# First tiles and first weight slices prepared one stage ahead in a three-layer transformer kernel on one core

## The reference

```
for l in range(2):                                   # first block
    mod = silu(c) @ w_ada[l] + b_ada[l]              # shift, scale, gate
    h = layer_norm(x) * (1 + scale) + shift
    u, v, z_a, q, k, val, z_b, q_idx, k_idx, w_idx = split(h @ w_in[l])
    y_a = silu(z_a) * spatial_gating_unit(u, v, ...)
    # q, k, q_idx, k_idx get a rotary embedding
    y_b = silu(z_b) * sparse_attention(q, k, val, q_idx, k_idx, w_idx)   # top 256 keys by index score
    x = layer_norm(ALPHA * x + gate * (concat(y_a, y_b) @ w_out[l]), ln_g, ln_b)
h = rms_norm(x, norm_pre)                            # second block
aq, ak, av, az, dq, dk, dv, db, da, dz, ga, gn = split(h @ w_in_2)
# dense attention on rms-normed, rotated aq, ak; a bidirectional gated delta rule on dq, dk, dv;
# both gated, summed, multiplied by w_out_2, normalised and added to x; a gated side input p is added last
```

## Time and profile before

| | |
|---|---|
| median of three runs | 3689.68 us |
| the profiled execution | 3680.2 us |
| its span (first to last instruction) | 3678.2 us |
| TensorE matmul busy | 3138.2 us, 85% |
| VectorE busy | 2146.1 us, 58% |
| ScalarE busy | 1372.8 us, 37% |
| GpSimd busy | 1140.9 us, 31% |
| bytes moved by DMA | 306.24 MB, 83 GB/s over the span |

### The profile page before, as it was taken

How to read it: one execution, slowest core, us unless ns; L and a number is a source line. 1 busy time by engine, 2 the same in 40 slices (tenths; PEclk the granted TensorE clock), 3 DMA queues, 4 the chain that set the end, 5 groups by cost and what they waited for, 6 DMA issues and landing times. The chain is left out here.

```text
span 3678.2 us, 43621 instructions
## 1 busy us (share of the span) xinstructions
PE 3138.2 (85%) x15729; PEld 2536.9 (69%) x15729; DVE 2146.1 (58%) x4123; ACT 1372.8 (37%) x2729; POOL 1140.9 (31%) x1248
## 2 busy tenths in 40 slices
PE   4899878868998788598998998968878688899788
PEld 3578645645776456487887886768867688688567
DVE  5699787556996876576772005457755577101223
ACT  1366345213763551235662212444323443121221
POOL 1236311221462113422004242225422344423310
PEclk9999999989998999799999999989989799899899
DMA  5322411531223125410002113123231331412511
GB/s 199 123 78 92 131 44 55 172 127 52 78 90 128 44 63 175 150 41 6 1 1 95 49 63 117 31 56 89 48 109 29 73 80 46 158 49 103 174 66 46
DMA packets 233337, 306.24 MB, mean 83 GB/s; under 512 B 40959, under 2 KB 149247, under 8 KB 230945
## 3 DMA queue, kind: packets, MB, share of 16 engines
q1 hardware_dynamic: 221602, 282.47, 24.8%
q10 hardware_dynamic: 11520, 20.98, 1.6%
HBM read 243.48 MB, written 59.90 MB: 82 GB/s over the span
## 5 line engine op out<-in xcount | busy, mean ns | idle before, releaser
L669 PE MATMUL psum<-qs,hT 128*128 128x512 f32 x1344 | 308.7, 391 | 9.5 <-POOL qs L756 9.3
L2342 PE MATMUL psum<-hTs,cws 128*128 128x512 f32 x1152 | 284.3, 408 | 33.2 <-POOL hTs L2589 29.5
L669 PEld LDWEIGHTS psum<-qs,hT 128*128 128x128 f32 x1344 | 252.5, 189 | 65.6 <-POOL qs L756 7.6
L2342 PEld LDWEIGHTS psum<-hTs,cws 128*128 128x128 f32 x1152 | 226.3, 198 | 82.8 <-POOL hTs L2589 30.3
L2093 PE MATMUL psum<-bhsn,bringn 128*128 128x512 f32 x1152 | 264.8, 392 | 14.1 <-POOL bringn L2138 13.3
L2093 PE MATMUL psum<-bhsa,bringa 128*128 128x512 f32 x1152 | 264.1, 392 | 9.4 <-POOL bringa L2138 9.4
L2093 PEld LDWEIGHTS psum<-bhsn,bringn 128*128 128x128 f32 x1152 | 217.7, 189 | 61.1 <-issue 13.6
L2093 PEld LDWEIGHTS psum<-bhsa,bringa 128*128 128x128 f32 x1152 | 218.1, 189 | 55.4 <-issue 9.8
L1403 PE MATMUL psum<-w_out,oys 128*128 128x512 f32 x768 | 180.0, 396 | 27.2 <-DVE w_out L1462 25.6
L1403 PEld LDWEIGHTS psum<-w_out,oys 128*128 128x128 f32 x768 | 146.6, 192 | 61.3 <-DVE w_out L1462 27.2
L836 DVE TENSOR_SCALAR_CACHE_REDUCE junk<-score,cand 128x384 uint8<-128x384 f32 x248 | 186.8, 810 | 2.2
(11 more groups left out here) (449 smaller groups left out, 6998.0 us busy)
## 6 DMA issues: line engine op xcount, KB each, us to landing
stg<-in_w_in SPq DMA_DIRECT2D x96, 256.0 KB, 2.7
wa<-in_w_ada SPq DMA_DIRECT2D x32, 512.0 KB, 3.5
pj<-ptmp ACTq DMA_DIRECT2D x64, 256.0 KB, 2.2
dlb<-blocks SPq DMA_DIRECT2D x32, 512.0 KB
dlb<-in_w_in SPq DMA_DIRECT2D x24, 512.0 KB, 3.9
wa<-in_w_ada SPq DMA_DIRECT2D x8, 1024.0 KB, 8.5
oyf<-yTd SPq DMA_DIRECT2D x16, 512.0 KB, 4.7
ostg<-in_w_out SPq DMA_DIRECT2D x16, 512.0 KB, 6.0
```

What stands on the lines that cost most here:

```text
L669: mm = pe.matmul(bank(m), lhs, rhs, start=(kc == 0 and x == 0), stop=(kc == KC - 1 and x == 2))
L2342: mm = pe.matmul(ps[:, u % 4, :], ws[c % 2][:, a, kc, :], hs[:, b, kc, half * HALF:(half + 1) * HALF], start=(kc == 0 and x == 0), stop=(k ...
```

## The change

The first tile of an index-inputs stage and that stage's weights are now fetched, normalised, turned and modulated in the stage ahead of it. For layer 0 that is the conditioning stage, for layer 1 the first-output stage of layer 0. A new class `FirstTile` holds the buffers and the steps. The first two tiles of the attention inputs and the 8 slices of their first weight chunk are prepared in the first-output stage of layer 1, by a new class `InputsAhead`; there, tile 0 is fully split and its turned form stored, and tile 1 is only normalised. Names are kept alive across the stages by an `ExitStack` called `early`, on the other side of the memory.

With it go: in the first-output stage of layer 1 the buffers `yf` and `ys` are three in place of four; the attention inputs have four staging buffers in place of three; the two `wa` buffers of the index inputs lie in `h.score`; and `recycle_semaphores` runs ahead of each first-output stage and once more after the second, three times in place of two.

```diff
+class FirstTile:
+    def load_w(self, sp):
+        w = self.k.t["w_in"][self.l].rearrange("(k p) n -> p k n", p=P)
+        sp.dma_start(self.w_qi[:, :, :], w[:, :, QI0:KI0]).then_inc(self.s_w, 16)
+        sp.dma_start(self.w_sm[:, :, 0:2 * HD], w[:, :, K0:ZB0]).then_inc(self.s_w, 16)
+        sp.dma_start(self.w_sm[:, :, 2 * HD:], w[:, :, KI0:D_IN]).then_inc(self.s_w, 16)
...
+class InputsAhead:
+    def load_w(self, sp, v):
+        if v >= 4:
+            sp.wait_ge(self.s_wlo, v - 3)
+        sp.dma_start(self.raw[v % 4], self.k.t["w_in_2"][0, v * P:(v + 1) * P, AK0:AK0 + HALF]).then_inc(self.s_w[v % 4], 16)
...
 stage_conditioning
             for kc in range(2, KC):
                 cd.load(sp, kc)
+            first.load_x(sp, k.t["x"][0])
+            first.load_w(sp)
...
             cd.sum_columns(pe, 0, ps[:, 5, 0:2 * KC])
+            first.turn(pe)
...
+            act.wait_ge(cd.s_kept, 1)
+            first.modulate(act)
...
             for kc in range(2, KC):
                 cd.accumulate(dve, kc)
+            first.stats(dve)
+            first.normalise(dve)
...
 stage_first_output
+        YF = YS = 3 if ahead else 4
...
+                if first and n == 3:
+                    sp.wait_ge(s_st[0], 16)
+                    first.load_x(sp, x_out)
+                    first.load_w(sp)
+                if ahead and n == 3:
+                    sp.wait_ge(s_st[0], 16)
+                    sp.wait_ge(s_wlo, KC)
+                    ahead.load_x(sp, 0)
+                    ahead.load_npre(sp)
+                    for v in range(4):
+                        ahead.load_w(sp, v)
+                if ahead and n == 4:
+                    sp.wait_ge(s_st[1], 16)
+                    ahead.load_x(sp, 1)
+                if ahead and n in (5, 6):
+                    ahead.load_w(sp, 2 * n - 6)
+                    ahead.load_w(sp, 2 * n - 5)
...
             def y_hi(n):
                 act.wait_ge(s_yl[n % YF], 16 * (n // YF + 1))
-                if n >= SLOTS:
-                    act.wait_ge(s_mm, n - SLOTS + 1)
+                if n >= YS:
+                    act.wait_ge(s_mm, n - YS + 1)
...
+                if ahead and 3 <= n < 7:
+                    ahead.w_lo(pool, 2 * n - 6)
+                    ahead.w_lo(pool, 2 * n - 5)
+                if ahead and 4 <= n < 6:
+                    ahead.rstd(pool, n - 4)
...
 stage_attention_inputs
-    SLICES, STAGING = CH * KC, 3
+    SLICES, STAGING = CH * KC, 4
...
-            turn_x(0)
             turn_x(1)
...
                 for kc in range(KC):
-                    if n == 0:
-                        pe.wait_ge(s_wlo, c * KC + kc + 1)
+                    if n == 0 and c:
+                        pe.wait_ge(s_wlo, (c - 1) * KC + kc + 1)
...
 build
-                stage_first_output(k, l, x_in, t["x1"] if l == 0 else t["x2"])
                 k.recycle_semaphores()
+                if l + 1 < DEPTH:
+                    tile0, inputs = FirstTile(k, early, l + 1), None
+                else:
+                    tile0, inputs = None, InputsAhead(k, early)
+                stage_first_output(k, l, x_in, t["x1"] if l == 0 else t["x2"], tile0, inputs)
+            k.recycle_semaphores()
```

More of the change, by code:

```diff
@@ L225, in stage_conditioning @@
+def stage_conditioning(k, first):
     nc, t, ps = k.nc, k.t, k.ps
@@ L255, in _ @@
             cd.clear(pool)
+            first.rstd(pool)
         @block.tensor
@@ L312, in stage_index_inputs @@
     with ExitStack() as ctx:
-        xb = [h.score[:, i * D:(i + 1) * D] for i in range(XB)]
+        xb = [first.x[:, :], h.score[:, 0:D]]
         xn = xb
-        hf = [h.score[:, (2 + i) * D:(3 + i) * D].rearrange("p (c q) -> p c q", c=KC) for i in range(2)]
-        w_qi = k.sb(ctx, f"w_qi_{l}", [P, KC, HALF])
-        w_sm = k.sb(ctx, f"w_sm_{l}", [P, KC, SMALL])
+        hf = [first.hf[:, :, :], h.score[:, D:2 * D].rearrange("p (c q) -> p c q", c=KC)]
+        wa = [h.score[:, (2 + i) * D:(3 + i) * D] for i in range(2)]
+        w_qi, w_sm = first.w_qi, first.w_sm
         st = k.sb(ctx, f"st_{l}", [P, 2, 2, 6])
@@ L407, in project @@
                 if n == 0:
-                    pe.wait_ge(s_w, 48)
+                    pe.wait_ge(first.s_w, 48)
                 if n >= 2:
@@ L1334, in _, with stage_first_output @@
                 gate(v)
-def stage_first_output(k, l, x_in, x_out):
+def stage_first_output(k, l, x_in, x_out, first, ahead):
     nc, t, ps = k.nc, k.t, k.ps
@@ L1376, in _ @@
                     s_wl[kc % STAGING], 16)
-            for n in range(LEAD, YF):
+            for n in range(LEAD, LEAD + 1):
                 load_y(n)
@@ L1420, in _ @@
                     part(n, kc)
+            if first:
+                pe.wait_ge(s_g, NT - SLOTS + 1)
+                first.turn(pe)
+            if ahead:
+                pe.wait_ge(s_g, NT - SLOTS + 1)
+                ahead.turn(pe)
         @block.scalar
@@ L1436, in _ @@
                 y_hi(n)
+                if ahead and n == NT - 2:
+                    ahead.square(act, 0)
+                    for v in range(4):
+                        ahead.w_hi(act, v)
+            if first:
+                first.modulate(act)
+            if ahead:
+                ahead.square(act, 1)
+                for v in range(4, KC):
+                    ahead.w_hi(act, v)
+                ahead.scale(act)
         @block.gpsimd
@@ L1464, in _ @@
             for n in range(NT + 1):
+                if first and n == 6:
+                    first.stats(dve)
+                if first and n == 7:
+                    first.normalise(dve)
+                if ahead and 6 <= n < NT:
+                    ahead.normalise(dve, n - 6)
                 if n < NT:
@@ L1486, in _, with stage_attention_inputs @@
                                              ALU.add).then_inc(s_o, 1)
-def stage_attention_inputs(k, a):
+            if ahead:
+                ahead.split(dve)
+def stage_attention_inputs(k, a, ahead):
     nc, t, ps = k.nc, k.t, k.ps
```

341 lines of the change are left out of this document (218 added, 123 removed).

## The result

Beside each other on one chip the changed kernel took 3652.38 us (median of 4 runs, 3644.80 to 3660.35) and the kernel before 3691.09 us (4 runs, 3685.44 to 3700.91): a ratio of 0.9893, 95% interval 0.9862 to 0.9923, so 1.1% faster. The forecast was 3652 us, faster. The profiled execution of the changed kernel took 3650.61 us with a span of 3648.7 us, 29.5 us less than the span of before.

What follows compares the result with a forecast made beforehand. TensorE, busy for 85% of the span, was taken as the bound, with gains only where it stands still or runs at half rate. 7.2 + 8.2 + (26.4 - 2 - 1.8) = 38.0 us off 3689.7 gave 3651.7, range 3637 to 3669.

Steps and rivals of the forecast that it cites:

- parts 4 and 5: First output of layer 1, a loss of 2 us; attention inputs up to the last low part, a gain of 26.4 us.
- parts 2 and 3: First output of layer 0 ends 3.5 us later; layer 1's index inputs start with net gain 8.2 us, that loss included.
- the forecast's term: Layer 0's index-inputs start: the turn stays on the path at 1.97 us, as slow as in the kernel before.
- The wait: First output of layer 0: VectorE stands at x tile 5 until 746.5 us, behind the early loads; tile 5 loses 9 us.
- part 2: First output of layer 0: early loads and new normalising end the stage 3.5 us later, bounds 0 and 8.
- VectorE has idle time at each tile here: First output of layer 1: reason for taking a loss of 2 us although low parts can stretch VectorE.
- The bound: First output of layer 1: upper loss of 9 us, with eight low parts each pushing one VectorE instruction, up to 7.6 us.
- the dates of the head roots: Attention inputs: roots of units 0 to 3 at 13.5, 20.6, 28.3, 34.9 us; last low part ends at 37.4.
- the slices stay slow: Attention inputs: cold TensorE units and VectorE's head norms pace the slices; gain there 18 us, time 3660, chance 0.12.
- part 4: First output of layer 1: three buffers, eight low parts and early loads cost 2 us, bounds 1 and 9.
- The slower rival: Slices loaded ahead: a loop of loads, stores and roots outweighs the gain; loss 45 us, time 3697, chance 0.03.
- sign of being wrong: TensorE idle over 3 us ahead of tile 7 in either output stage, or attention inputs' last slice later than 45 us.

Runs made afterwards that it cites:

- loads_behind: Changed kernel with the early loads of both first-output stages one round later, behind y tile 7 and x tile 5: 3653.72 us, ratio 0.9899.
- three_y: Kernel before with three yf and ys buffers in layer 1's first output and one recycling more ahead of each first output: one profile, 3690.83 us.
- early_slices: Changed kernel with the eight weight slices prepared at the beginning of layer 1's first output: 3652.15 us, ratio 0.9899.
- sum_first: Changed kernel with VectorE's head sums ahead of the rotation tables for the attention inputs' first six units: 3652.13 us, ratio 0.9897.
- low_written: Changed kernel with GpSimd writing zeros instead of subtracting for the attention inputs' low parts, so the output lacks them: one profile, 3640.36 us.
- the three edits: Changed kernel with later early loads, slices at layer 1's first-output beginning, and head sums before tables: 3646.21 us (0.9882), again 3644.31 us (0.9879).

## Why the prediction was right, and where it was not

The forecast of 3652 us met the median of the first four runs, and the mechanism was right too: three starts shortened, and the rest of the program shifted by as much. That the time agrees to 0.4 us is luck. The stretches sum to 34.4 us, not 38.0, with parts 4 and 5 worse and parts 2 and 3 better than forecast; and the first four runs beside each other happened to show 38.7, where all runs show 34.4.

1. *First start:* 7.7 against 7.2. The turn and the modulation cost what the earlier trace rows gave. The turn behind the 32 matmuls of one column took 1.95 us, as slow as the 1.97 before, where a later one took 1.04, so the forecast's term held. The projection took 8.59 us against 9.23, but between 8.6 and 10.2 over the profiles of this study.
2. *First output, layer 0:* 1.7 against 3.5. The wait was rightly placed, and the transfers took what was forecast: 16.2 us from the first of the early loads to the landing of x tile 5, where the forecast had 17.0. Two steps were off. The early loads were issued 69.4 us after the stage's first load, and the forecast put them at the 71.3 of the y load in the trace of before; so x landed 2.7 us earlier in the stage than forecast. And TensorE's tile 7 was to start 1.6 us late, but the low part of y tile 7 was ready in time. loads_behind shows that the wait is the whole cost.
3. *Layer 1's start:* 10.4 against 8.2, of which 1.8 is the better part 2 and 0.3 the recycling, 1.4 to 1.5 us where I took 1.8.
4. *First output, layer 1:* 4.3 against 2, within its bounds. TensorE's idle time was as forecast (1.4 us, three_y). The step that failed is "VectorE has idle time at each tile here". Three of the four pairs of low parts stretched two scalings by 1.1 to 1.2 us together. Idle time absorbed most of the first two, and VectorE takes the last tile up 0.9 us late; the last pair meets VectorE in the tail, behind TensorE's last tile, where nothing idles. early_slices gave 2.1 us back. The bound, one pushed instruction for each of eight low parts, was too high.
5. *Attention inputs:* 21.9 against 26.4, the one term that was off by more than 3 us. The step that failed is the dates of the head roots. I had them at 13.5, 20.6, 28.3 and 34.9 us; they came at 14.8, 22.8, 33.0 and 42.0. Each round came 1 to 2.5 us later than I had counted, by two things: the tables stand ahead of the sum in each unit, so that the root waits for them (sum_first: the last low part 6.4 us earlier), and VectorE's instructions are stretched beside the low parts (low_written: 27.7 us of work are 17.2). The rival "the slices stay slow" named the right mechanism, VectorE's chain of head norms, and priced it at 18 us; the truth lay between it and my forecast. I had priced that stretching only in part 4, and had looked there at the eight low parts that leave this stage, not at the sixteen that stay in it.

The slower rival did not come near: TensorE had no idle time ahead of tile 7 in either output stage. Neither sign of being wrong appeared, since the last slice came before 45 us.

## What to carry to other kernels

Work that is moved ahead is free where the engines that take it are idle, not where they are idle on average: put it into the idle time at the beginning of a stage, not into its last tile, where no matmul covers VectorE any more. When a stream through several engines gets more buffers, look for the engine that answers last in each round, and move what it need not do first behind its answer. And take a gain from stretches between fixed rows of two traces: one untouched stretch of this program differs by up to 13 us from run to run, as much as the three edits gained.

## What the runs showed of the hardware

- VectorE's two-input instructions wait for GpSimd's subtractions but not for its writes: pairs of products that take 0.49 and 0.76 us alone took 2.65 and 2.95 beside subtractions, and the pair of 0.49 took 0.49 beside writes.
- SyncE can be held by its own issue. Of the four loads in a row for the next stage (3.3 MB) the last, the 72 columns of `w_sm`, took 4.62 us to issue, and the load of y behind it 3.04 in place of 0.5; with the loads one round later it was 5.48 us, and 3.22 for the store behind it. At its old places, also behind x and the other weights, the same load took 3.83 and 4.70 us to issue. Whether the bytes ahead of it or its own short rows do this was not tried.
- A recycling of the semaphores with its two barriers costs 1.4 to 1.6 us when it is added at a stage border (2.84 us without, 4.2 to 4.4 with it).
- Identical code differs between executions by stretches, not evenly. Layer 0's stretch took 604.2, 609.9 and 601.5 us in three profiles of the changed kernel, layer 1's 598.0, 597.3 and 598.2; over all profiles it was 601.5 to 609.9 and 594 to 599. What makes the first vary was not tried.
